# Five modulation sets moved to earlier layers, sums of squares on VectorE, modulation columns ahead of the last residual

## The reference

```python
for i in range(4):
    shift1, scale1, gate1, shift2, scale2, gate2 = split(silu(c) @ ada_w[i] + ada_b[i], 6)
    h = x * (1 + scale1) + shift1
    y = mixer_i(h)            # conformer, hgrn2, mlstm (matrix memory), stick-breaking attention
    x = layer_norm(8 ** 0.25 * x + (1 + gate1) * y, g[i, 0], b[i, 0])
    h = x * (1 + scale2) + shift2
    y = (silu(gate) * val) @ ffn_w_down[i]   # gate, val: causal conv of h @ ffn_w_up[i]
    x = layer_norm(8 ** 0.25 * x + (1 + gate2) * y, g[i, 1], b[i, 1])
```

## Time and profile before

| | us |
|---|---|
| median of 3 runs | 2522.26 |
| lowest, highest | 2513.01, 2531.91 |
| profiled execution | 2514.33 |
| its span, first to last instruction | 2512.5 |
| granted TensorE clock, mean over the span | 0.973 of full |
| PE busy, DVE busy, ACT busy | 2327.8, 1946.5, 1434.3 |

### The profile page before, as it was taken

The page is one execution under the profiler, slowest core; times in us unless marked ns, Lnnn a source line. Parts: engine busy times, 40 slices in busy tenths (PEclk is TensorE's granted clock), DMA queues, the critical chain, the costliest instruction groups (busy, mean ns, idle before and its releaser), DMA issues. The chain is left out here.

```text
span 2512.5 us, 45699 instructions
## 1 busy us (share of the span) xinstructions
PE 2327.8 (93%) x18446; PEld 2217.1 (88%) x18446; DVE 1946.5 (77%) x3441; ACT 1434.3 (57%) x2652; POOL 12.8 (1%) x20
## 2 busy tenths in 40 slices
PE   8899999989999998889998889999988999888998
PEld 7899999978899998779987889988778999766998
DVE  6578798757687986968888778885568888856885
ACT  7635564465355645467645767656554765534764
POOL 0000000000000000000000000000000000000000
PEclk9999999999999999999999999999989999989999
DMA  6215578713175785125575435663515558622552
GB/s 249 88 51 208 196 279 316 294 68 135 62 257 197 291 335 216 53 82 188 202 285 218 185 118 197 228 246 118 189 47 201 177 193 305 255 93 74 195 187 100
DMA packets 64226, 463.36 MB, mean 184 GB/s; under 512 B 7248, under 2 KB 7440, under 8 KB 8208
## 3 DMA queue, kind: packets, MB, share of 16 engines
q1 hardware_dynamic: 64016, 460.44, 49.3%
HBM read 459.37 MB, written 1.05 MB: 183 GB/s over the span
## 5 line engine op out<-in xcount | busy, mean ns | idle before, releaser
L761 PE MATMUL psum<-arena_rounded,upper_rounded 128*128 128x256 f32 (+1 forms) x4792 | 1357.0, 283 | 83.0 <-DVE ring_rounded L572 28.9
L762 PE MATMUL psum<-arena_rounded,upper_rounded 128*128 128x256 f32 (+1 forms) x4792 | 1340.3, 280 | 0.0
L763 PE MATMUL psum<-arena_rounded,ring_rounded 128*128 128x256 f32 (+1 forms) x4792 | 1340.0, 280 | 0.0
L572 DVE TENSOR_TENSOR ring_rounded<-ring,upper_rounded 128x1024 fp32r<-128x1024 f32 (+4 forms) x958 | 836.8, 896 | 248.6 <-ACT upper_rounded L563 244.2
L563 ACT ACTIVATE upper_rounded<-ring 128x1024 fp32r<-128x1024 f32 (+4 forms) x958 | 750.1, 795 | 475.7 <-PE psum L763 378.9
L761 PEld LDWEIGHTS psum<-arena_rounded,upper_rounded 128*128 128x128 f32 (+1 forms) x4792 | 911.2, 190 | 102.7 <-issue 59.3
L762 PEld LDWEIGHTS psum<-arena_rounded,upper_rounded 128*128 128x128 f32 (+1 forms) x4792 | 911.3, 190 | 1.3 <-issue 0.5
L763 PEld LDWEIGHTS psum<-arena_rounded,ring_rounded 128*128 128x128 f32 (+1 forms) x4792 | 911.9, 190 | 0.0
L587 DVE CUSTOM_DVE_ANT_0 ring<-ring,silu_c,cols 128x1024 f32<-128x1024 f32 x192 | 244.4, 1277 | 0.0
L2519 DVE SCALAR_TENSOR_TENSOR arena<-psum,cols,arena 128x255 f32<-128x255 f32 (+1 forms) x352 | 153.2, 477 | 53.0 <-ACT arena L2486 49.9
L2486 ACT ACTIVATE arena<-psum,cols 128x256 f32<-128x256 f32 x176 | 89.4, 560 | 69.1 <-PE psum L763 67.7
(11 more groups left out here) (519 smaller groups left out, 2530.0 us busy)
## 6 DMA issues: line engine op xcount, KB each, us to landing
ring<-stream_dram SPq DMA_DIRECT2D x434, 1024.0 KB, 4.9
const<-const_dram SPq DMA_DIRECT2D x1, 1540.0 KB, 14.8
x<-x_dram SPq DMA_DIRECT2D x1, 1024.0 KB, 4.8
out_dram<-x SPq DMA_DIRECT2D x4, 256.0 KB, 2.0
cols<-cols_dram SPq DMA_DIRECT2D x1, 974.0 KB, 11.5
silu_c<-c_dram SPq DMA_DIRECT2D x1, 512.0 KB, 15.6
const<-const_dram SPq DMA_DIRECT2D x1, 67.0 KB, 4.7
pos<-positions_dram SPq DMA_DIRECT2D x1, 64.0 KB, 6.0
```

What stands on the lines that cost most here:

```text
L572: dve.tensor_tensor(self.chip.rounded(raw), raw, self.chip.whole(upper), ALU.subtract).then_inc(self.lower_ready, 1)
L761: pe.matmul(out, upper, x[0][:, b.k, :], start=(b.k == 0), stop=False)
L762: pe.matmul(out, upper, x[1][:, b.k, :], start=False, stop=False)
L763: ins = pe.matmul(out, lower, x[0][:, b.k, :], start=False, stop=(b.k == nk - 1))
```

## The change

The sets 0 and 6 now ride in `mla_o` of the two first layers in place of a third set in `down`; `ml_x` gets two sets and `ml_z` two in place of none and one, and `ffn_down` of layers 0 to 2 has one in place of two. In `add_and_center` the squares are added on DVE in all eight calls, and both matmuls of sums stand behind the last block of the projection. The modulated gain and bias (three operations on 8 columns) are made before the last `take` in place of behind the variance, those of the residual (two operations) at the end. DVE writes h itself only for feature tiles 0 and 1 (before: 0 to 3); for the others ACT does.

```diff
                                         [[(h * P + D_NOPE, (h + 1) * P) for h in range(H_MLA)]]))
-        g["mla_o", l] = by_rounds(matrix("mla_w_o", (l,), H_MLA * D_V, tiles(0, KD)))
+        g["mla_o", l] = with_sides(by_rounds(matrix("mla_w_o", (l,), H_MLA * D_V, tiles(0, KD))), sides(1))
         kvr = OFF_RW + W_RW, OFF_RW + 2 * W_RW, OFF_RW
...
         g["up", l] = with_sides(by_rounds(matrix("w_up", (l,), D, tiles(0, F1 // P)), TOGETHER), sides(2))
-        g["down", l] = with_sides(by_rounds(matrix("w_down", (l,), F1, tiles(0, KD))), sides(3))
+        g["down", l] = with_sides(by_rounds(matrix("w_down", (l,), F1, tiles(0, KD))), sides(2))
     for i in range(L2):
...
             raw = [headwise_weights(m) for m in range(K_ML)]
-            g["ml_x", i] = with_raw(by_rounds(matrix("ml_w_up_2", (0,), D, tiles(0, K_ML)), TOGETHER),
+            g["ml_x", i] = with_raw(with_sides(by_rounds(matrix("ml_w_up_2", (0,), D, tiles(0, K_ML)), TOGETHER), sides(2)),
                                     {t: raw[t - ML_LAG] for t in range(ML_LAG, K_ML)})
-            g["ml_z", i] = with_raw(with_sides(by_rounds(matrix("ml_w_up_2", (0,), D, tiles(I_ML, K_ML))), sides(1)),
+            g["ml_z", i] = with_raw(with_sides(by_rounds(matrix("ml_w_up_2", (0,), D, tiles(I_ML, K_ML))), sides(2)),
                                     {t: raw[K_ML - ML_LAG + t] for t in range(ML_LAG)})
...
         g["ffn_down", i] = with_sides(by_rounds(matrix("ffn_w_down_2", (i,), F2, tiles(0, KD))),
-                                      sides(2 if i + 1 < L2 else 0))
+                                      sides(1 if i + 1 < L2 else 0))
     assert next(ada, None) is None
...
     following = (i, 1) if j == 0 else (i + 1, 0)
-    on_dve = nk > KD
     end = KD - 1
...
-    def sum_squares(pe, ks):
-        for k in ks:
-            pe.wait_ge(squared, k + 1)
-            pe.matmul(power, chip.con("ones"), squares[:, k, :], start=(k == 0), stop=False)
-
-    def sum_rest(pe):
-        pe.wait_ge(rest_summed, end - 1 - CENTRE)
-        pe.matmul(offset, chip.con("ones"), rest_sum, start=True, stop=False)
-        if on_dve:
-            pe.wait_ge(squares_summed, end - 1)
-            pe.matmul(power, chip.con("ones"), square_sum, start=True, stop=False)
-        else:
-            sum_squares(pe, (end - 2, end - 1))
-
     def statistics(pe):
         ones = chip.con("ones")
+        pe.wait_ge(rest_summed, end - 1 - CENTRE)
+        pe.matmul(offset, ones, rest_sum, start=True, stop=False)
+        pe.wait_ge(squares_summed, end - 1)
+        pe.matmul(power, ones, square_sum, start=True, stop=False)
         pe.wait_ge(free, KD)
...
-    inserts = {(CENTRE + 1, 0): sum_first, (end, nk - 2): sum_rest}
-    if not on_dve:
-        inserts[end - 1, nk // 2] = lambda pe: sum_squares(pe, range(0, 3))
-        inserts[end, 1] = lambda pe: sum_squares(pe, range(3, end - 2))
+    inserts = {(CENTRE + 1, 0): sum_first}
...
                                bias=h_bias[:, k:k + 1]).then_inc(upper_ready, 1)
-                if k >= KD // 2:
+                if k >= 2:
                     act.activation(lower[:, k, :], xs[:, k, :], ACT.Identity, scale=h_gain[:, k:k + 1],
...
+            def modulation():
+                add, scale = (ada_col(chip, following[0], 3 * following[1] + which, 0, KD) for which in (0, 1))
+                w.wait_modulation(dve, following[0], 3 * following[1] + 1)
+                dve.tensor_tensor(h_gain, gain, scale, ALU.mult)
+                chain(dve.tensor_tensor(h_bias, shift, scale, ALU.mult))
+                chain(dve.tensor_tensor(h_bias, h_bias, add, ALU.add), bias_ready)
+
             for n in range(steps):
...
                     w.dve(dve, s["last"] - 2)
-                    if on_dve:
-                        add_squares(end - 2)
-                        add_squares(end - 1)
+                    add_squares(end - 2)
+                    add_squares(end - 1)
+                    if not last:
+                        modulation()
                 take(n)
...
                     add_rest(end - 1)
-                    for m in range(1, end - 2 if on_dve else 1):
+                    for m in range(1, end - 2):
                         add_squares(m)
...
             recentre(1)
-            if not last:
-                add, scale = (ada_col(chip, following[0], 3 * following[1] + which, 0, KD) for which in (0, 1))
-                w.wait_modulation(dve, following[0], 3 * following[1] + 1)
-                dve.tensor_tensor(h_gain, gain, scale, ALU.mult)
-                chain(dve.tensor_tensor(h_bias, shift, scale, ALU.mult))
-                dve.tensor_tensor(h_bias, h_bias, add, ALU.add)
-                dve.tensor_scalar(x_gain, gain, ALPHA, None, ALU.mult)
-                chain(dve.tensor_scalar(x_bias, shift, ALPHA, None, ALU.mult))
-            for k in range(2, KD // 2):
-                recentre(k)
             dve.wait_ge(root_ready, 2)
             def lower_of(k):
                 dve.wait_ge(upper_ready, k + 1)
-                if k >= KD // 2:
-                    dve.wait_ge(whole_ready, k + 1 - KD // 2)
+                if k >= 2:
+                    dve.wait_ge(whole_ready, k - 1)
                 dve.tensor_tensor(chip.rounded(lower[:, k, :]), lower[:, k, :], chip.whole(upper[:, k, :]),
                                   ALU.subtract).then_inc(lower_ready, 1)
             for k in range(KD):
-                if k >= KD // 2:
+                if k >= 2:
                     recentre(k)
                 dve.wait_ge(recentred, k + 1)
                 dve.tensor_tensor(xs[:, k, :], xs[:, k, :], rstd, ALU.mult).then_inc(normed, 1)
                 if last:
                     continue
-                if k < KD // 2:
+                if k < 2:
                     dve.wait_ge(normed, k + 1)
...
             if not last:
+                dve.tensor_scalar(x_gain, gain, ALPHA, None, ALU.mult)
+                chain(dve.tensor_scalar(x_bias, shift, ALPHA, None, ALU.mult))
                 lower_of(KD - 1)
```

## The result

The change makes the kernel slower by less than 1%. Thirteen runs of each on the same chip: 2516.71 us before (2510.67 to 2531.91) and 2537.12 after (2529.56 to 2541.71), ratio 1.0074, interval 1.0059 to 1.0089; that is +18.6 us, from 14.8 to 22.4. The forecast was 2529, in a range of 2510 to 2546. Slower by less than 1%, as forecast, and in the range; the sum of +8.6 was less than half of what came. Part of the nearness of 2529 is luck: it stands on the median of three runs, 2522.26, where thirteen give 2516.71. On that base the same sum gives 2525.3, and the measured 2537.12 is 11.8 above it.

What follows compares the result with a forecast made beforehand. PE was taken to bound the kernel. Terms 6.0 + 3.3 - 2.5 - 4.3 + 1.1 - 1.4 + 6.4 = +8.6 us gave 2530.9 from the three-run median; forecast 2529, range 2510 to 2546.

Steps and rivals of the forecast that it cites:

- `mla_o`, +6.0 and 3.0 of clock: Sets into `mla_o`: PE restarts 2.6 us later in layer 0, 3.4 in layer 1; slow clock behind both waits, 2 x 1.5.
- The loads cost nothing either: In `mla_o`: six-slot ring holds two weight and four side units, first slot free before the attention; cost 0.
- The forecast wait at L625, 4.2 us: Behind `mla_o`: PE's wait at the stage end would be near 4.2 us in both layers.
- `down`, 0: Set leaving `down`, both layers: no PE wait worth a row there, so worth 0, at most a few tenths.
- `ml_x`, 0: Sixteen pieces into `ml_x`: two fit a tile's idle DVE time, three overrun by 1.2 to 2, carried onward; cost 0.
- So there is a little room: Loads in `ml_x`: 6.8 MB in 20.9 us, an estimated 325 GB/s, beside 312 GB/s at a share of 0.82.
- My rival for `ml_x`: In `ml_x`, DVE's work exceeds the tile, all sixteen pieces on the path: 19.4 us more, +28, 2550; chance 0.07.
- `ml_z`, +3.3 and 1.0 of clock: In `ml_z`: early wait 1.2 us shorter, PE's wait for the series grows to 6.2; slow clock behind it 1.0.
- `ffn_down`, -2.5: Sets leaving `ffn_down` 0 to 2: two stalls of 1.37 and 1.11 us go; each stage's starting stall stays.
- The norm, -4.3 + 1.1 - 1.4 = -4.6: Layer norms, us: earlier last take -4.3, three calls getting DVE's adds +1.1, opening of the next projection -1.4.
- The clock, +6.4: Slow clock behind new or longer PE waits, us: `mla_o` 2 x 1.5, `ml_z` 1.0, three norms 0.8 each.
- The rival "the clock takes more": Clock falls last about twice as long, three norms pay in full: +11.6 on top, +20, 2542 us; chance 0.16.

Runs made afterwards that it cites:

- e12b: Changed kernel with one part undone: no set in `mla_o`, three again in `down`; +4.0 us against the kernel before.
- e3: Kernel before with the whole changed layer norm alone, every conditioning set where it was; -4.5 us against the kernel before.
- e6: Kernel before with the `mla_o` sets moved from `down`, plus seven matmuls of constants filling PE's wait behind `mla_o`; +12.3 us against the kernel before.
- e2: Kernel before with only the set moves of `ml_x`, `ml_z` and `ffn_down` 0 to 2; +6.0 us against the kernel before.
- e7: Kernel before with two sets in `ml_x` alone, `ffn_down` 0 and 1 having one instead of two; +5.3 us against the kernel before.
- e1: Kernel before with only one set moved from `down` to `mla_o` in both layers; +11.8 us against the kernel before.
- e4: Kernel before with half the changed norm: modulation and opening moved, sums and squares as before; +2.3 us against the kernel before.
- e8: Changed kernel with matmuls of constants filling five PE waits (three norms, behind `mla_o`, in `ml_z`); +6.0 us against the kernel before.
- e5: Kernel before with the whole changed norm, plus five matmuls of constants in each of PE's three new norm waits; -5.0 us against the kernel before.
- e9b: Kernel before with two sets in `ml_x`, starting two tiles later, and `ffn_down` 0 and 1 relieved; -0.5 us against the kernel before.
- e10b: Kernel before with changed norm, its waits filled, one set moved from `ffn_down` 0 to `hg_g`, one from `ffn_down` 1 to late `ml_x`; -1.0 us.

## Why the prediction was right in sign and short in size

**`mla_o`, +6.0 and 3.0 of clock: too small, 9.0 against 11.8 to 14.6.** The failed step is one sentence: "The loads cost nothing either: the ring of six holds the two weight units and four side units". The first slot is not free before the attention; the next load is issued at the first conversions of `mla_o` (97.8 in layer 0, 577.2 in layer 1). From e12b to the changed kernel, in their traces, `mla_o` costs 7.3 in layer 0 and 7.1 in layer 1. In layer 0 0.9 of it passes in the attention (forecast 0.8), and PE's restart moves from

```profile
107.67 0.36 PE L761 MATMUL psum<-arena_rounded,upper_rounded 128*128 128x256 f32 x1 [1.67 <-PEq L625]
```

to 112.01; since e12b had been 0.9 behind at the start of the attention, that is 5.2 by waits where 2.6 was forecast. The 2.6 between them has the size of DVE's idle time for the late load, 2.15, and of the 2.3 by which DVE's work there outlasts the sum; no piece is as long. The rest, 2.1, is clock (forecast 1.5). The forecast wait at L625, 4.2 us, was met by 4.52 and 3.70, but from a later stage end: a right number there did not prove the sum.

**`down`, 0: right.** At first I read 3.8 us of gain in layer 1 from the traces before and after. It is not the sets: in e3, where they stay, 2.4 of it is there too, in e6, where they are gone, nothing of it is, and it belongs to the two paces told of below.

**`ml_x`, 0: wrong, about +5.** That is what three traces show when they are followed through the stage: 5.6 in the changed kernel, 4.9 in e2, 5.0 in e7. The run of e7, +5.3, says only that `ml_x` with the relief of `ffn_down` 0 and 1 costs between 0.5 and 10.3. "So there is a little room" was an average rate over four tiles, 325 GB/s; the loads come in bursts. In e2 the load that ACT waits 5.4 us for was issued at 1710.0, 0.7 behind another, with the transfer engines full, and took 7.9 us to land; the next one was issued only at 1722.0, and between the two the engines stood idle:

```profile
1712.00:1716.00 4.00, 4.00 (x32) 3.87 (x31) 3.96 (x9) 0.54 (x2) 0.00 (x0) 1.00 0.97 406
1716.00:1720.00 4.00, 0.95 (x10) 0.36 (x8) 2.12 (x4) 2.02 (x10) 0.00 (x0) 1.00 0.03 8
```

So both count, when a slot comes free and what else is issued with it. I also took the tile from its steady part, with one conversion; the second and third tiles have two and had no idle time at all. My rival for `ml_x` had the place, but the wrong resource and a price four times too high.

**`ml_z`, +3.3 and 1.0 of clock: right by the traces; no run has it alone.** The early stall fell from 2.35 to 1.15, the wait grew to 5.88; followed through both traces the stage costs 4 to 5.

**`ffn_down`, -2.5: right in sign, size open.** From before to e2, `ffn_down` 0 gains 2.5, more than the stall that I had named (1.37), as another got shorter too; `ffn_down` 1 gains 4.4 and `ffn_down` 2, for which nothing was forecast, 3.0. But in each of these two the trace before has one stretch of half clock, 3.4 us, more than e2, and e1, which leaves all three as they were, gains 1.9 in `ffn_down` 1. In the changed kernel one stall of 1.13 stays in `ffn_down` 1, where there were 1.60 and 1.11.

**The norm, -4.3 + 1.1 - 1.4 = -4.6, with 2.4 of clock -2.2: right within the interval.** e3 measures -4.5 [-8.1 to -0.8], which can't tell -4.6 from -2.2. From before to e3 the end of `ffn_down` 0 gains 1.4 (forecast 1.0 and 0.2 for the opening); e4 shows that the squares and the sums bring it.

**The clock, +6.4: too small.** About 16 by the mean clocks, 23 in the profiled pair; e8 gives 12.6 back. I priced one short stretch per wait. In `mla_o` layer 0 and in `ml_z` it lasts longer:

```profile
1835.80:1841.70 5.90, 0.02 (x2) 0.01 (x1) 5.76 (x11) 4.34 (x10) 0.00 (x0) 0.86 0.76 301
1841.70:1850.00 8.30, 8.30 (x30) 7.08 (x31) 4.78 (x7) 2.65 (x6) 0.00 (x0) 0.50 0.19 56
```

Here PE was busy for all of 8.3 us and still at half speed. Others come and go in code that nothing changed. PE's wait of 2.2 us at the start of `ffn_down` 0 (1253 us in the kernel before, 1270 in the changed one) is the same in both, and only in the changed one is it followed by 3.4 us at half clock. The scores of layer 1, at 533 to 552 us, are at half clock for 3.4 or 6.8 us in every trace but that of the kernel before: there it is this one execution that was lucky, and the code that it runs from 402 to 552 us takes 3.0 to 6.8 us longer in each of the eight other traces (e2 to e5, e7, e9b, e10b, e12b) that have the same code there. The rival "the clock takes more", 2542, thus came nearer to 2537 than the forecast, and its +20 on the base of thirteen runs, 2516.71, gives just 2537. Its rule from the Trainium skill, "TensorE: Matmul & The Clock Gate", section "HAM oscillation — how this bites in real kernels", that waits between bursts let the clock fall anew, is borne out by these rows, by e6's stretch and by e8; as the 2.2 us above show, the same wait does not always do it. That rival deserved more than 0.16, though part of its nearness is luck too: it has no term for the loads. Which of the five fills gives e8 its 12.6 stays open; no run separates parts of 2 to 4 us.

## What to carry to other kernels

Work that is moved on one engine brings its operands with it. Ask of a prefetch ring not whether it holds the units, but when each slot comes free and how long a load takes to land from there: a side unit ahead of a weight unit holds a slot, and issued together with it lands first. And where an engine must wait anyway, count the wait and the slow stretch behind it apart; a few idle matmuls can pay for the second (12.6 us in e8, nothing that the runs show in e5 and e6), not for the first.

## What the runs showed of the hardware

**Two paces of the same matmul at the same granted clock.** Matmuls of TensorE by line, 40 us of `ffn_up` 3 at clock 1.00, in the kernel before and in e2, which runs identical code there:

```profile
L761 PE MATMUL psum<-arena_rounded,upper_rounded 128*128 128x256 f32 x119 | 32.8, 276 | 0.0
```

```profile
L761 PE MATMUL psum<-arena_rounded,upper_rounded 128*128 128x256 f32 x114 | 32.0, 281 | 0.0
```

119 against 114 in the same time: PE starts one every 113 ns or one every 118, for tens to hundreds of us on end, and both paces occur in every trace. In `down` of layer 1 (40 us each, kernel before, then the changed one):

```profile
920.00:960.00 40.00, 40.00 (x342) 40.00 (x341) 30.83 (x42) 15.85 (x21) 0.00 (x0) 1.00 0.88 347
```

```profile
900.00:940.00 40.00, 40.00 (x355) 40.00 (x355) 28.66 (x38) 17.31 (x22) 0.00 (x0) 1.00 0.73 287
```

By an estimate from the spacing of matmuls at full clock, the slow pace costs some 14 us in the trace before and 20 in that of e2. It moved 4 us of one profiled pair to a stage where nothing was won. What chooses it is open; a comparison of single traces should count matmuls per time in unchanged code first.

**A load of 1 MB takes 4.8 us alone, 6.9 at the median when six follow each other** (share 1.01, 420 to 424 GB/s): in a burst each later unit is late by what stands before it.
